# A two-layer decoder step: retrieved expert rows regrouped as 32 tokens by four slots, and all their weighted sums on TensorE

## What is computed

```python
PEER_HEADS = 8; N_KEYS = 128; PEER_TOPK = 16        # 8 x 16 = 128 experts for each token
def one(xb):                                         # xb: tokens x 1024
    qh = (xb @ wq).reshape(blk, PEER_HEADS, 2, PEER_HALF)
    s = jnp.einsum('thcd,hcnd->thcn', qh, keys)
    ...                                              # two top-16, their 256 sums, the best 16: eidx, g
    act = gelu(einsum('thkd,td->thk', u[eidx], xb))
    return einsum('thk,thkd->td', g * act, v[eidx])
```

## Time and profile before

| | |
|---|---|
| median of the runs | 5584.86 us |
| span of the profiled execution | 5599.6 us |
| TensorE busy with matmuls | 4306.3 us, 77% |
| VectorE busy | 3537.3 us, 63% |
| GpSimd busy | 2480.1 us, 44% |
| ScalarE busy | 1216.0 us, 22% |
| moved by DMA | 1484.67 MB, mean 265 GB/s |
| mean granted TensorE clock | 0.870 |

### The profile page before, as it was taken

How to read it: one execution, slowest core, us unless ns; L and a number is a source line. 1 busy time by engine, 2 the same in 40 slices (tenths; PEclk the granted TensorE clock), 3 DMA queues, 4 the chain that set the end, 5 groups by cost and what they waited for, 6 DMA issues and landing times. The chain is left out here.

```text
span 5599.6 us, 50197 instructions
## 1 busy us (share of the span) xinstructions
PE 4306.3 (77%) x15868; PEld 2641.6 (47%) x15868; DVE 3537.3 (63%) x7830; ACT 1216.0 (22%) x3039; POOL 2480.1 (44%) x2215
## 2 busy tenths in 40 slices
PE   7956886578577988689677676968678798767777
PEld 6334775543333765263334565554344476223333
DVE  4055638866677546686666848966667754854544
ACT  2042311121332112120422311121242211111111
POOL 0000010166555544546565332456555554477776
PEclk9975997689789999799898888988889899888888
DMA  4311631389787987889889966688888798799999
GB/s 141 118 60 41 229 124 61 118 294 349 269 272 267 334 284 272 278 308 371 290 292 323 339 203 199 203 286 323 306 274 274 264 359 281 249 361 409 409 409 361
DMA packets 579390, 1484.67 MB, mean 265 GB/s; under 512 B 60104, under 2 KB 251176, under 8 KB 572616
## 3 DMA queue, kind: packets, MB, share of 16 engines
q0 software_dynamic: 307200, 1115.82, 55.2%
q1 hardware_dynamic: 258968, 331.39, 17.8%
q10 hardware_dynamic: 12960, 34.26, 1.6%
HBM read 1435.37 MB, written 45.93 MB: 265 GB/s over the span
## 5 line engine op out<-in xcount | busy, mean ns | idle before, releaser
L2721 PE MATMUL duo<-vring,diag 128*128 128x512 f32 (+1 forms) x2976 | 1509.2, 657 | 401.1 <-DMA vring<-in_peer_v,eidx 173.2
L2593 POOL DMA_INDIRECT uring<-in_peer_u,eidx x981 | 1140.5, 1163 | 1112.3 <-DVE uring L2629 658.0
L2674 POOL DMA_INDIRECT vring<-in_peer_v,eidx x1024 | 1134.0, 1107 | 1067.0 <-PE duo L2721 472.7
L2721 PEld LDWEIGHTS duo<-vring,diag 128*128 128x128 f32 (+1 forms) x2976 | 589.6, 208 | 1197.3 <-issue 944.6
L2629 DVE SCALAR_TENSOR_TENSOR uring<-uring,xr 128x1024 f32<-128x1024 f32 x795 | 958.9, 1221 | 204.6 <-DMA uring<-in_peer_u,eidx 178.8
L689 PE MATMUL duo<-wx,xT 128*128 128x512 f32 (+3 forms) x1440 | 605.1, 578 | 32.9 <-PEq L133 32.1
L2754 DVE SCALAR_TENSOR_TENSOR x_tok<-vring,wt,x_tok 128x1024 f32<-128x1024 f32 x296 | 385.0, 1301 | 97.0 <-DMA vring<-in_peer_v,eidx 70.4
L2702 ACT ACTIVATE diag<-ident,wt 128x128 f32<-128x128 f32 x728 | 269.8, 395 | 748.4 <-PE duo L2721 678.8
L689 PEld LDWEIGHTS duo<-wx,xT 128*128 128x128 f32 (+1 forms) x1440 | 238.9, 176 | 385.8 <-issue 383.1
L2629 DVE SCALAR_TENSOR_TENSOR uring<-uring,duo 128x1024 f32<-128x1024 f32 x201 | 245.4, 1221 | 264.4 <-DMA uring<-in_peer_u,eidx 263.9
L533 PE MATMUL duo<-xT,wx 128*128 128x264 f32 (+1 forms) x1536 | 357.6, 397 | 36.5 <-ACT newcols L556 30.6
(11 more groups left out here) (472 smaller groups left out, 5283.8 us busy)
## 6 DMA issues: line engine op xcount, KB each, us to landing
wx<-in_w_in SPq DMA_DIRECT2D x32, 2048.0 KB
wx<-in_w_in SPq DMA_DIRECT2D x48, 1024.0 KB, 8.3
wm<-in_w_in SPq DMA_DIRECT2D x32, 1024.0 KB, 10.4
wm<-in_w_branch_a SPq DMA_DIRECT2D x32, 1024.0 KB, 11.6
wq<-in_peer_wq SPq DMA_DIRECT2D x32, 1024.0 KB, 8.7
tokm<-tout ACTq DMA_DIRECT2D x64, 256.0 KB
eb<-decays SPq DMA_DIRECT2D x32, 512.0 KB, 4.5
s_h<-in_state_ssm SPq DMA_DIRECT2D x16, 1024.0 KB, 8.3
```

The costliest lines, as they stand in the source:

```text
L2593: pool.indirect_dma_start(out=E.rings.urows[K % E.ur], out_offset=None, in_=table, in_offset=bass.IndirectOffsetOnAxis(ap=E.tiles[q][3][:, ...
L2674: pool.indirect_dma_start(out=E.rings.vrows[K % E.vr], out_offset=None, in_=table, in_offset=bass.IndirectOffsetOnAxis(ap=E.tiles[q][3][:, ...
L2721: mm = pe.matmul(G.bank[6 + c][0:m, :], G.diag[:, R % DR, 0:m], E.rings.vrows[K % E.vr][:, c * BANK:(c + 1) * BANK], start=first, stop=las ...
```

## The change

The gathered block of a slot now holds 32 tokens with four of their experts each: partition 32k + i holds expert k of token i of a sub-block of 32 tokens. A tile still has 128 such slots, in packs of four (`PACK`), one slot for each sub-block. The stationary operand is a 128x32 matrix (`G.subsel` times the weights), which adds the four experts of a token, and its output goes to the 32 PSUM partitions of the sub-block, so that the four slots of a pack are four 32-column tiles of the array. All slots are summed on TensorE; `SHARES`, `assign`, the folds on VectorE and `copy_rows` are gone. The rings are four and four (`UR` 5 to 4; five and 18 in `last`). The V job waits for, sums and frees a whole pack at a time. The token rows are loaded for each sub-block, four times over (four `xr` buffers of 512 KB per tile where there was one). Numbers and gates have to be re-dealt to the new places: SyncE does it with 16 small DMAs for each tile, and the routing stage waits for them at its end. `PLAN_DOTS` and `PLAN_SUMS` are as before.

```diff
-UR, VR, DR = 5, 4, 4
+UR, VR = 4, 4
+PACK = 4
+SUB = P // PACK
+DEAL = SLOTS // PACK
+DR = 2 * PACK
...
+        @block.sync
+        def _(sp):
+            go = G.beside.by(sp, "SP")
+            G.ahead.fetch(sp, 0, *vectors)
+            for i, (t, n, heads, sc) in enumerate(units):
+                go(ends[i])
+                sp.wait_ge(sem("routed"), i + 1)
+                if t < NT:
+                    for j in range(PACK):
+                        for k in range(PACK):
+                            sp.dma_start(G.routed[k * SUB:(k + 1) * SUB, t, :, j * DEAL:(j + 1) * DEAL],
+                                         B.dealing[j * SUB:(j + 1) * SUB, :, k * DEAL:(k + 1) * DEAL]).then_inc(sem("dealt"), 16)
...
+            sp.wait_ge(sem("dealt"), dealt[-1])
...
 def dots_sync(sp, E):
...
+        for b, rows in zip(tile.buffers, tile.subs):
+            at = E.before(q, b)
+            if at is not None:
+                yield at + 1.5
+            if E.k0 or at is not None:
+                sp.wait_ge(G.dotted, E.k0 + (0 if at is None else at + 1))
+            sp.dma_start(G.xr[:, b, :], rows).then_inc(G.xrow[b], 16)
...
 def sums_pool(pool, E):
...
         if k >= E.vr:
-            freed(k - E.vr)
+            pool.wait_ge(G.summed, E.p0 + (k - E.vr) // PACK + 1)
...
     for v in range(E.n - E.vr):
-        yield v + 1.0
+        yield float(v // PACK * PACK + PACK)
         down(v + E.vr)
...
 def sums_tensor(pe, E):
...
+    for v in range(0, E.n, PACK):
+        yield float(v + PACK)
...
+        pe.wait_ge(G.diagged, E.k0 + v + PACK)
+        for i in range(v, v + PACK):
+            K = E.r0 + i
+            pe.wait_ge(E.rings.vsems[K % E.vr], 16 * (K // E.vr + 1))
         for c in range(2):
-            mm = pe.matmul(G.bank[6 + c][0:m, :], G.diag[:, R % DR, 0:m], E.rings.vrows[K % E.vr][:, c * BANK:(c + 1) * BANK],
-                           start=first, stop=last, skip_group_check=True)
+            for i in range(v, v + PACK):
+                j = E.slots[i][1]
+                mm = pe.matmul(G.bank[6 + c][tile.out(j), :], G.diag[:, (E.k0 + i) % DR, 0:m],
+                               E.rings.vrows[(E.r0 + i) % E.vr][:, c * BANK:(c + 1) * BANK],
+                               start=j < (PACK if tile.dealt else 1), stop=j >= tile.slots - (PACK if tile.dealt else 1), skip_group_check=True)
         mm.then_inc(G.summed, 1)
```

More of the change, by code:

```diff
@@ L18 @@
 SEQ, DECB = 512, 8
+QUAD = 32
 NT = SEQ // P
@@ L2511, in __init__, with buffer, column, out @@
         self.urows, self.vrows, self.usems, self.vsems, self.shared = urows, vrows, usems, vsems, shared
+class Tile:
+    def __init__(self, t, n, slots, rows, gates, sel, subs):
+        self.t, self.n, self.slots, self.rows, self.gates, self.sel, self.subs = t, n, slots, rows, gates, sel, subs
+        self.dealt = len(subs) > 1
+        self.buffers = list(range(PACK)) if self.dealt else [PACK - 1]
+    def buffer(self, j):
+        return self.buffers[j % len(self.buffers)]
+    def column(self, j):
+        return j % PACK * DEAL + j // PACK if self.dealt else j
+    def out(self, j):
+        return slice(j % PACK * SUB, (j % PACK + 1) * SUB) if self.dealt else slice(0, self.n)
+    def gates_of(self, lo, hi):
+        if not self.dealt:
+            return self.gates[:, lo:hi]
+        return self.gates.rearrange("p (j s) -> p s j", j=PACK)[:, lo // PACK:hi // PACK, :]
+    def slots_of(self, row, lo, hi):
+        return row[:, lo:hi].rearrange("p (s j) -> p s j", j=PACK) if self.dealt else row[:, lo:hi]
 class Experts:
@@ L2537, in __init__ @@
         self.dots_end, self.sums_end = float(self.n + 1 + WEIGH_AFTER), float(self.n)
[L2538 to L2559, removed]
     @property
@@ L2565, in later, with before, loads @@
     def later(self):
-        n = sum(self.on_pe)
-        return (self.k0 + self.n, self.g0 + len(self.ends), self.q0 + len(self.pe_tiles), self.p0 + n, self.d0 + self.n - n)
+        return self.k0 + self.n, self.g0 + len(self.ends), self.q0 + len(self.tiles), self.p0 + self.n // PACK
+    def before(self, q, b):
+        for p in range(q - 1, -1, -1):
+            tile = self.tiles[p]
+            if b in tile.buffers:
+                return self.first[p] + tile.slots - len(tile.buffers) + tile.buffers.index(b)
+        return None
+    def loads(self, q, b):
+        return self.xr0[b] + sum(b in tile.buffers for tile in self.tiles[:q]) + 1
     def need(self, v):
@@ L2571, in need @@
         lo = j // self.size * self.size
-        return self.first[q] + min(lo + self.size, self.tiles[q][2]) + 1.0 + WEIGH_AFTER
+        return self.first[q] + min(lo + self.size, self.tiles[q].slots) + 1.0 + WEIGH_AFTER
     def ready(self, v):
@@ L2619, in dots_vector @@
             q, j = E.slots[i]
[L2620 to L2626, removed]
+            tile = E.tiles[q]
+            K, b = E.r0 + i, tile.buffer(j)
+            if j < len(tile.buffers):
+                dve.wait_ge(G.xrow[b], 16 * E.loads(q, b))
             dve.wait_ge(E.rings.usems[K % E.ur], 16 * (K // E.ur + 1))
             row = E.rings.urows[K % E.ur]
-            dve.scalar_tensor_tensor(row, row, 1.0, xr, ALU.mult, ALU.mult,
+            dve.scalar_tensor_tensor(row, row, 1.0, G.xr[:, b, :], ALU.mult, ALU.mult,
                                      accum_out=G.pre[:, q % 2, j:j + 1]).then_inc(G.dotted, 1)
@@ L2975 @@
              {"ssd": 16, "ssmout": 7, "qkv": 9, "attn0": 30, "attn1": 34, "mix": 40, "norm2": 6, "pscore": 27, "route": 29, "route2": 26})
-SHARES = {"tokproj": 1.0, "ssd": 0.3, "attn0": 0.35, "attn1": 0.35, "mix": 0.8, "norm2": 0.5, "pscore": 1.0, "last": 0.0, "last_end": 0.5}
-def spans(E, order, dots, sums):
-    ahead = Beside()
-    lead, job = Job({}, E, E.dots_end, dots, order), Job({}, E, E.sums_end, sums, order)
-    ahead.begin("U", lead)
-    ahead.begin("V", job)
-    out = []
-    for key in order:
-        ahead.open(key, {})
-        out.append((key, job.now, job.goal))
-    return out
 def rope_table():
```

201 lines of the change are left out of this document (82 added, 119 removed).

## The result

The changed kernel takes 6299.53 us (median of four runs, 6290.1 to 6303.87) against 5588.09 us before (median of four runs; 5584.86 is that of the first three of them): ratio 1.127, 95% interval [1.125, 1.129]. It is slower, as forecast, but by 711 us where 77 were forecast, and outside the range.

The account below looks back on a forecast made before the run. V's ring was taken to decide. Stages with V +14, re-deal +33, token rows +12, U's ring +15 and last pack +3 gave +77 on 5599.6 us; less 14.7 for the profiled run, 5660 us, range 5470 to 5960.

Parts of the forecast that it names:

- the ring as the term that decides: V's ring of four buffers, freed together, sets the pace of stages with V: 3.1 us for each slot.
- Lockstep: In V's ring, nothing is gathered while TensorE sums a pack, and nothing can be summed while the next is gathered.
- their sum of +14: Stages with V: inputs +53, `pscore` +21, routing +27, `vectors` +11, chunks -40, outputs -14, attention -50, `mix` +6; us.
- the token rows: Three more 0.5 MB loads for each of eight tiles, 31 us of transfer, about 40% in full stretches: +12 us.
- U's ring: Ring of U from five to four buffers: 0 to 17 us for each of three `tokproj`, 5 taken: +15 us.
- the column tiles: V's sums on TensorE: four column tiles run at once, a pack's 16 matmuls lasting about 1.9 us.
- two at a time: Rival for V's sums: only two column tiles run together, 3.5 us for each slot, 5955 us; chance 0.14.
- tiles in turn: Rival for V's sums: column tiles run one by one, 4.4 us for each slot, about 6500 us; chance 0.04.
- the turn, as the term of 12.4 us: V's ring: issues 3.7, landing 6.3, sums 1.7, semaphores and tiling 0.6; 3.1 us for each slot, bounds 2.75 and 3.5.
- The landing: In V's ring, the last of four gathers lands in 6.3 us, against a 5.3 median in a routing stage.
- the step from turn to stage: Stages with V: new length is slots times 3.1 us where that is above what the other work needs.
- the re-deal: 16 small DMAs at routing's end, 11 us for each tile, four of eight tiles exposed: +33 us net.

Follow-up runs that it names:

- b_free4: The kernel before, with V's buffers waited for and refilled in fours and nothing else changed: 6367.55 us, ratio 1.140.
- step2: The changed kernel with V waiting, summing and freeing in steps of two slots instead of four: 5983.49 us, ratio 1.071.
- half8: The changed kernel with token rows loaded by four DMAs, V gathering half rows into eight buffers (two packs): 5618.2 us, ratio 1.005.
- x16_step2: The changed kernel with each token-row load as four DMAs of 32 rows, and V in steps of two slots: 5843.55 us, ratio 1.046.
- x16: The changed kernel with each token-row load as four DMAs of 32 rows instead of one with outermost dimension four: 6143.89 us, ratio 1.100.
- x2: The changed kernel with each token-row load as two DMAs whose outermost dimension is two: 6417.69 us, ratio 1.148.
- b_ur4: The kernel before with U's ring at four buffers instead of five: 5648.51 us, ratio 1.011.

## Why the prediction was wrong

**Right: the direction, and the ring as the term that decides.** Lockstep was named with its mechanism, and b_free4, step2 and half8 show it. What failed is its price and that of two smaller terms: the stages with V came out some 430 us above their sum of +14, the token rows 144 above their 12, and U's ring 49 above its 15. The first two overlap by some 34 us, the token rows' part in the routings.

**Right: the column tiles.** Four run at the same time. Timeline of TensorE in `pscore` after:

```profile
2257.63 1.92 PE L2743 MATMUL duo<-vring,diag 128*32 128x512 f32 x16
2259.48 0.33 PE L2298 MATMUL duo<-ident,pk 128*128 128x128 f32 x1
```

16 matmuls in 1.92 us, forecast 1.9, where 16 in turn took 7.13. The rivals of two at a time and of tiles in turn are out, though the second's time (6500) was the nearest.

**Wrong: the turn, as the term of 12.4 us.** At the full clock the shortest turns are 11.6 us, in `pscore`. But the clock was at its lower level in most stretches with V: 0.56 in a routing that had 0.85, 0.60 in attention inputs that had 1.00. A pack there is 3.6 us instead of 1.9. I had this 1.7 and put it "inside the bounds" instead of into the sum; turns are 13.5 us in the routing, which is 3.4 for each slot. The landing, with semaphores, was priced too high: 6.9 us in the sum, 5.9 from the last issue to TensorE's start and 0.3 behind the pack in the rows. With the clock's 1.7 alone added it would have been 14.1.

**Wrong: the step from turn to stage.** I set a stage to the larger of its slots times the turn and its other work. In the routing with 59 slots this holds: 15 turns of 13.1 to 15.6 us fill 207 of its 215.2 us, where I forecast 183, and the miss is the turn. Elsewhere it doesn't hold. Attention on the fourth tile took 134.0 us with 36 slots, 3.7 us each, where I forecast 105; the six attention stages came out at +95 against -50, the chunks at +30 against -40, the output stages at 0 against -14, the three routings at +199 against +27. The steps of a pack stand in TensorE's program order between steps of the foreground: a pack can wait for the foreground ahead of it (once it started 13.9 us after its last gather was issued, in attention on the fourth tile, against 5.1 to 6.5 in the routing), and its gathers for the pack, and the foreground behind it waits for the gathers. In attention on the fourth tile TensorE waited 47.6 us for gathered rows (12.5 before), and foreground starts where such a wait and its pack end:

```profile
1922.43 3.59 PE L2743 MATMUL duo<-vring,diag 128*32 128x512 f32 x16 [11.93 <-DMA vring<-in_peer_v,routed]
1925.95 1.98 PE L1173 MATMUL duo<-kT,a_qT 64*128 64x512 f32 x4
```

I read it so that the two lengths partly add; that each such step was ready before is not shown. Even x16_step2, with a finer ring, needs 187.7 us for the routing that takes 162.6.

How the some 430 us divide is an estimate: 0.3 us more for each of some 650 slots outside `mix` and `tokproj` is about 190; the token rows (34 by x16) and the re-deal (up to 34) lie inside the routings; some 170 are left for the lengths that add.

The attention inputs came out at +39 (forecast +53), `vectors` at +16 (+11), `mix` at +5 (+6), and `pscore` at +26 and +31 (+10 each). That the attention inputs came out below the forecast is no merit of it: with the longer turn they summed 48 slots where they had summed 54, and the other six fell to the neighbours. For `pscore` I priced TensorE and the ring each at 84 us and took the larger; half8, which has no lockstep, shows 85.7, and the rest up to 99.7 is again the two together.

**Wrong: the token rows, 12 us for their bytes.** x16 shows 156 us or more. I counted bytes and not how the access is laid out, and none of the queue behind it: in `norm1` the prefetch of weights is held by 25 us. The rule was at hand (see x2), and so was the access with its outermost dimension of four, which x16 takes out.

**Wrong: U's ring, 15 us.** It is 64 (b_ur4). My bound of 0 to 17 for each `tokproj` held the measured 13 to 21 nearly, and I took 5; it misses 5 to 6 us in each `xbc` and 4 to 5 in each store stage.

**Right: the re-deal.** 11.3 us in the first routing, forecast 11. For the other exposures no run tells it alone.

An account by runs: 156 (token rows) + 300 to 316 (pairs instead of fours, with what the clock gives back) + 64 (U's ring) leave some 180 of the 711 us. `pscore` and `mix` with full TensorE are about 86 of it in x16_step2's stages (24, 3 and 24; 18, 1 and 17), the four re-deals up to 45, the token-row issues still ahead of the weights in `norm1` 17. Some 30 us stay open.

## What to carry to other kernels

When work is grouped to make an engine faster, count the ring in groups: a ring of one group is no ring, however many buffers it has, and what counts is gathers in flight while the group is computed. Freeing four buffers together in a ring of four, with no other change, cost 14% (b_free4). Steps that share an engine's program order with a chain of foreground steps add to it when they wait, so the larger of the two lengths is a lower bound and not a forecast. Price a changed load by the outermost dimension of its access and by what is queued behind it, before its bytes.

## What was not expected of the hardware

Four 32-column tiles of float32 matmuls run fully side by side: 1.92 us for 16, 3.7 times faster than in turn; the Trainium skill ("TensorE: Matmul & The Clock Gate", Part 3) has 2.38x for three. Loads of token rows with an outermost dimension of four or two, in place of 32, slow the stage that waits behind them from 23 to 41 and 58 us.
